# Neighbourhood attention with the scale in the queries' norm, the bias and maxima in PSUM, and the value product turned round

## The reference, cut to what matters

```
q, k, v = split(h @ w_qkv);  q = rms_norm(q, q_g);  k = rms_norm(k, k_g)      # per head
s_loc = (q . k) * 64**-0.5 + bias      # bias: a table by row and column distance,
s_loc = where(col_mask, s_loc, -1e30)  #       -1e30 outside a window of 16 columns
s_ctx = (q . k_c) * 64**-0.5
p = softmax(concat(s_loc, s_ctx))      # 512 probabilities to a query
o = p_loc @ v + p_ctx @ v_c
y = merge(o) @ w_o
```

## Time and profile before

| | |
|---|---|
| median of 3 runs | 1802.4 us |
| lowest, highest | 1801.71, 1804.6 us |
| the profiled execution | 1802.83 us |
| its span | 1801.0 us |
| mean granted TensorE clock | 0.963 of 2.4 GHz |
| PE, PEld busy | 94%, 82% |
| DVE, ACT, POOL busy | 56%, 42%, 5% |
| the attention | from about 1496 to 1572.8 us of the span |

### The profile page before, as it was taken

One profiled execution on the slowest core, in us unless ns is written; L12 is line 12 of the kernel. 1 busy time (PEld: TensorE's weight loads), 2 busy tenths in 40 slices (PEclk: granted clock), 3 DMA queues, 4 the chain that ended last, 5 costly groups with the idle time before them and its releaser, 6 DMA issues.

```text
span 1801.0 us, 29404 instructions
## 1 busy us (share of the span) xinstructions
PE 1685.1 (94%) x11903; PEld 1476.6 (82%) x11903; DVE 1000.8 (56%) x1205; ACT 749.6 (42%) x1100; POOL 95.8 (5%) x70
## 2 busy tenths in 40 slices
PE   6989999989989999959998999999979998789998
PEld 6988998979979989858786888888858784589998
DVE  5687556557785665464246443444353228866574
ACT  4444554344445544344225332233233234645453
POOL 0110000002000000020002000000020101110000
PEclk9999999989999999969998999999989998989999
DMA  7665665756756656612122323332323323145753
GB/s 241 214 208 189 210 204 174 252 177 210 231 174 205 211 190 212 231 45 94 47 70 70 94 72 94 111 95 79 88 94 117 100 71 71 24 128 172 205 173 120
DMA packets 329970, 259.69 MB, mean 144 GB/s; under 512 B 24018, under 2 KB 322386, under 8 KB 329827
## 3 DMA queue, kind: packets, MB, share of 16 engines
q1 hardware_dynamic: 311184, 251.55, 43.9%
q10 hardware_dynamic: 18642, 6.18, 1.6%
HBM read 256.65 MB, written 1.05 MB: 143 GB/s over the span
## 4 chain that ended last, share of the span: by engine, by line
PE 82%; DVE 10%; ACT 4%; issue 1%; POOL 1%; DMA 1%; ACTq 0%; SPq 0%; DVEq 0%
PE banks_g L1013 39%; PE banks_g L763 22%; PE banks_g L753 4%; PE banks_g L1001 3%; PE banks_g L785 2%; ACT near_p L1584 1%; PE bank_s L880 1%; PE bank_m L799 1%; DVE near_p L2006 1%; DVE near_max L2173 1%; PE bank_t L893 1%; DVE w_lo L1726 1%; POOL h L1662 1%; PE banks_g L745 1%; PE bank_o L907 1%
## 5 line engine op out<-in xcount | busy, mean ns | idle before, releaser
L1013 PE MATMUL banks_g<-h_hi,w_lo 128*128 128x512 f32 (+1 forms) x864 | 299.3, 346 | 9.7 <-DVE h_lo L2109 9.7
L1013 PE MATMUL banks_g<-h_lo,w_hi 128*128 128x512 f32 (+1 forms) x864 | 297.4, 344 | 0.0
L1013 PE MATMUL banks_g<-h_hi,w_hi 128*128 128x512 f32 (+1 forms) x864 | 297.3, 344 | 0.0
L1979 DVE TENSOR_TENSOR w_lo<-raw,w_hi 128x2048 fp32r<-128x2048 f32 (+1 forms) x100 | 207.7, 2077 | 158.5 <-ACT w_hi L1378 158.5
L1726 DVE TENSOR_TENSOR w_lo<-raw,w_hi 128x2048 fp32r<-128x2048 f32 x92 | 210.7, 2290 | 103.2 <-ACT w_hi L1219 103.2
L763 PE MATMUL banks_g<-h_hi,w_lo 128*128 128x256 f32 x832 | 241.3, 290 | 8.4 <-DVE h_lo L1967 8.4
L763 PE MATMUL banks_g<-h_lo,w_hi 128*128 128x256 f32 x832 | 236.2, 284 | 0.0
L763 PE MATMUL banks_g<-h_hi,w_hi 128*128 128x256 f32 x832 | 235.8, 283 | 0.0
L1378 ACT ACTIVATE w_hi<-raw 128x2048 fp32r<-128x2048 f32 (+1 forms) x100 | 173.3, 1733 | 74.1 <-DMA raw<-w_down 47.9
L1013 PEld LDWEIGHTS banks_g<-h_hi,w_lo 128*128 128x128 f32 x864 | 163.9, 190 | 33.6 <-DVE h_lo L2109 12.0
L1219 ACT ACTIVATE w_hi<-raw 128x2048 fp32r<-128x2048 f32 x96 | 182.9, 1905 | 6.9 <-issue 2.4
(11 more groups left out here) (306 smaller groups left out, 2907.0 us busy)
## 6 DMA issues: line engine op xcount, KB each, us to landing
raw<-w_in SPq DMA_DIRECT2D x76, 1024.0 KB, 5.1
ada_raw<-ada_w SPq DMA_DIRECT2D x48, 1024.0 KB, 7.2
raw<-w_up SPq DMA_DIRECT2D x88, 512.0 KB, 4.6
raw<-w_down SPq DMA_DIRECT2D x32, 704.0 KB, 4.4
raw<-w_branch SPq DMA_DIRECT2D x12, 1024.0 KB, 5.1
raw<-qkv SPq DMA_DIRECT2D x12, 1024.0 KB, 4.9
raw<-w_out SPq DMA_DIRECT2D x8, 1024.0 KB, 5.0
raw<-even_in SPq DMA_DIRECT2D x6, 1024.0 KB, 5.1
```

Source lines behind the costliest of these rows:

```text
L1013: last = nc.tensor.matmul(gb[:, m * SEQ:m * SEQ + nt], w[:, c, m0:m0 + P], a[:, c, 0:nt], start=c == 0 and n == 0, stop=c == kcs - 1 and n ...
L1979: nc.vector.tensor_tensor(w_lo[:, u % SLOTS, 0:n], raw[:, u % SLOTS, 0:n], w_hi[:, u % SLOTS, 0:n].bitcast(F32), ALU.subtract).then_inc(dv ...
```

## The change

Five things, in one edit:

1. The scale 1/8 moves into the queries' norm: the root is taken of sum + 64 eps in place of sum/64 + eps, for the queries alone.
2. The bias is added to the local scores in place in PSUM. The pass over the context scores goes. The maximum is taken from PSUM, and the exponentials read PSUM and write SBUF. So a score bank pair is free only after the exponentials (PE waits for `near exp` in place of `near masked`).
3. The probabilities are turned as they are, not normalised. The reciprocal is kept (4 buffers).
4. In the value product the turned probabilities (128 keys x 128 queries) are the stationary operand, and `v_n` (128 keys x 64 features) streams. The result is queries x features of both heads, in columns 0 to 127 of its bank.
5. VectorE multiplies that result (128 x 128) by the reciprocal into `near_o`; a new step **near back** on TensorE transposes it into columns 128 to 255 of the same bank, from where `f_hi` and `f_lo` are made as before. The pipeline is one batch deeper: scores b, turn b-2, back b-4, values b-3, exp b.

```diff
-    for b in range(19):
+    for b in range(20):
         if b < 16:
             order.append(("near scores", b))
         if 2 <= b <= 17:
             order.append(("near turn", b - 2))
-        if b >= 3:
+        if b >= 4:
+            order.append(("near back", b - 4))
+        if 3 <= b <= 18:
             order.append(("near values", b - 3))
@@ TensorE
                     if b >= 2:
-                        pe.wait_ge(dve_steps, dve_.at(f"near masked{b - 2}"))
+                        pe.wait_ge(act_steps, act_.at(f"near exp{b - 2}"))
...
-                    pe.wait_ge(dve_steps, dve_.at(f"near probs{b}"))
+                    pe.wait_ge(act_steps, act_.at(f"near exp{b}"))
...
-                    for kt in range(4):
-                        for e in range(2):
-                            hh = 2 * c + e
-                            last = nc.tensor.matmul(ob[64 * e:64 * e + 64, 0:P], v_n[:, kt, hh * HD:hh * HD + HD],
-                                                    near_pt[:, b % 2, kt, e, :], start=kt == 0, stop=kt == 3)
+                    for e in range(2):
+                        hh = 2 * c + e
+                        for kt in range(4):
+                            last = nc.tensor.matmul(ob[:, 64 * e:64 * e + 64], near_pt[:, b % 2, kt, e, :],
+                                                    v_n[:, kt, hh * HD:hh * HD + HD], start=kt == 0, stop=kt == 3)
...
+                elif what == "near back":
+                    b, = arg
+                    pe.wait_ge(dve_steps, dve_.at(f"near o{b}"))
+                    ob = bank_o if b % 2 == 0 else bank_g[0]
+                    nc.tensor.transpose(ob[:, P:2 * P], near_o[:, b % 2, :], ident[:, :]).then_inc(
+                        pe_steps, pe_.step(f"near back{b}"))
@@ ScalarE
-                        nc.scalar.activation(m_root[0:16, 0:nt], bank_m[0:16, 0:nt], ACT.Sqrt, scale=1.0 / HD,
-                                             bias=eps[0:16, 0:1]).then_inc(act_steps, act_.step(f"root{x}"))
+                        by, e_ = (1.0, eps_hd) if x == "q" else (1.0 / HD, eps)
+                        nc.scalar.activation(m_root[0:16, 0:nt], bank_m[0:16, 0:nt], ACT.Sqrt, scale=by,
+                                             bias=e_[0:16, 0:1]).then_inc(act_steps, act_.step(f"root{x}"))
...
                     act.wait_ge(dve_steps, dve_.at(f"near max{b}"))
+                    if b >= 3:
+
+                        act.wait_ge(pe_steps, pe_.at(f"near turn{b - 3} 1"))
                     for e in range(2):
-                        nc.scalar.activation(near_p[b % 3][:, e, :], near_p[b % 3][:, e, :], ACT.Exp,
+                        nc.scalar.activation(near_p[b % 3][:, e, :], near_banks(b)[:, e, :], ACT.Exp,
...
-                        ob[:, 0:P], ACT.Copy).then_inc(act_steps, act_.step(f"near hi{b}"))
+                        ob[:, P:2 * P], ACT.Copy).then_inc(act_steps, act_.step(f"near hi{b}"))
@@ VectorE
-                nc.vector.tensor_tensor(near_p[b % 3][:, :, :], near_p[b % 3][:, :, :],
-                                        near_inv[:, :].rearrange("p (e o) -> p e o", o=1).to_broadcast([P, 2, 512]),
-                                        ALU.mult).then_inc(dve_steps, dve_.step(f"near probs{b}"))
...
-                    nc.vector.scalar_tensor_tensor(pb[:, :, 0:SEQ], sbk[:, :, 0:SEQ], SCALE, backwards(bt),
-                                                   ALU.mult, ALU.add).then_inc(dve_steps, dve_.step("near"))
-                    nc.vector.tensor_scalar(pb[:, :, SEQ:512], sbk[:, :, SEQ:512], SCALE, None, ALU.mult).then_inc(
+                    nc.vector.tensor_tensor(sbk[:, :, 0:SEQ], sbk[:, :, 0:SEQ], backwards(bt), ALU.add).then_inc(
                         dve_steps, dve_.step(f"near masked{b}"))
+                    own()
+                    nc.vector.tensor_reduce(near_max[:, b % 2, :], sbk[:, :, :], AX.X, ALU.max, negate=True).then_inc(
+                        dve_steps, dve_.step(f"near max{b}"))
                     if b:
-                        near_normalize(b - 1)
-                    own()
-                    nc.vector.tensor_reduce(near_max[:, b % 2, :], pb[:, :, :], AX.X, ALU.max, negate=True).then_inc(
-                        dve_steps, dve_.step(f"near max{b}"))
+                        near_reciprocal(b - 1)
...
                 elif what == "near values":
+                    b, = arg
+                    ob = bank_o if b % 2 == 0 else bank_g[0]
+                    dve.wait_ge(pe_steps, pe_.at(f"near values{b}"))
+                    dve.wait_ge(dve_steps, dve_.at(f"near inv{b}"))
+                    nc.vector.tensor_tensor(near_o[:, b % 2, :].rearrange("p (e n) -> p e n", e=2),
+                                            ob[:, 0:P].rearrange("p (e n) -> p e n", e=2),
+                                            near_inv[:, b % 4, :].rearrange("p (e o) -> p e o", o=1).to_broadcast([P, 2, HD]),
+                                            ALU.mult).then_inc(dve_steps, dve_.step(f"near o{b}"))
```

More of the change, by code:

```diff
@@ L397, in program @@
         eps = sb("eps", [P, 1])
+        eps_hd = sb("eps_hd", [P, 1])
         x_t = sb("x_t", [P, KC, SEQ])
@@ L1594, in _ @@
                                                                              act_.step(f"near turned{b} {hf}"))
-                elif what == "near values":
+                elif what == "near back":
                     b, = arg
                     qt, c = divmod(b, KC)
-                    act.wait_ge(pe_steps, pe_.at(f"near values{b}"))
+                    act.wait_ge(pe_steps, pe_.at(f"near back{b}"))
                     ob = bank_o if b % 2 == 0 else bank_g[0]
@@ L1616, in _ @@
             nc.gpsimd.memset(eps[:, :], EPS).then_inc(pool_steps, pool_.step("eps"))
+            nc.gpsimd.memset(eps_hd[:, :], EPS * HD).then_inc(pool_steps, pool_.step("eps"))
             nc.gpsimd.memset(ones[:, :], 1.0).then_inc(pool_steps, pool_.step("ones"))
@@ L1999, in hidden_low, with near_reciprocal @@
                                         ).then_inc(dve_steps, dve_.step(f"f lo{ly} {i}"))
-            def near_normalize(b):
+            def near_reciprocal(b):
                 dve.wait_ge(act_steps, act_.at(f"near exp{b}"))
-                nc.vector.reciprocal(near_inv[:, :], near_sum[:, b % 2, :]).then_inc(dve_steps, dve_.step("near inv"))
-                own()
-                nc.vector.tensor_tensor(near_p[b % 3][:, :, :], near_p[b % 3][:, :, :],
-                                        near_inv[:, :].rearrange("p (e o) -> p e o", o=1).to_broadcast([P, 2, 512]),
-                                        ALU.mult).then_inc(dve_steps, dve_.step(f"near probs{b}"))
+                nc.vector.reciprocal(near_inv[:, b % 4, :], near_sum[:, b % 2, :]).then_inc(
+                    dve_steps, dve_.step(f"near inv{b}"))
             u = 0
@@ L2160, in _ @@
                     qt, c = divmod(b, KC)
[L2161 removed]
+                    sbk = near_banks(b)
                     dve.wait_ge(pool_steps, pool_.at(f"windowed{b // 2}"))
@@ L2165, in _ @@
                     bt = bias[b // 2 % 3][:, 2 * (c % 2):2 * (c % 2) + 2, :]
[L2166 to L2168 removed]
+                    nc.vector.tensor_tensor(sbk[:, :, 0:SEQ], sbk[:, :, 0:SEQ], backwards(bt), ALU.add).then_inc(
                         dve_steps, dve_.step(f"near masked{b}"))
+                    own()
+                    nc.vector.tensor_reduce(near_max[:, b % 2, :], sbk[:, :, :], AX.X, ALU.max, negate=True).then_inc(
+                        dve_steps, dve_.step(f"near max{b}"))
                     if b:
[L2171 to L2174 removed]
+                        near_reciprocal(b - 1)
                     if b == 15:
[L2176 removed]
+                        near_reciprocal(b)
                 elif what == "near values":
+                    b, = arg
[6 more added lines that the diff above has]
+                                            ALU.mult).then_inc(dve_steps, dve_.step(f"near o{b}"))
+                elif what == "near back":
                     b, = arg
@@ L2182, in _ @@
                     dve.wait_ge(act_steps, act_.at(f"near hi{b}"))
-                    nc.vector.tensor_tensor(v8(f_lo), ob[:, 0:P], v8(f_hi).bitcast(F32), ALU.subtract).then_inc(
+                    nc.vector.tensor_tensor(v8(f_lo), ob[:, P:2 * P], v8(f_hi).bitcast(F32), ALU.subtract).then_inc(
                         dve_steps, dve_.step(f"near lo{b}"))
```

6 lines of the change are left out of this document (2 added, 4 removed).

## The result

The change takes **1789.82 us** (median of 4 executions, 1783.28 to 1792.13) against 1803.39 for the kernel before on the same chip: ratio 0.992, 95% interval 0.9892 to 0.9947. The profiled one, 1783.28 us, is the lowest of the four, so what its trace shows beyond the attention is more than the median has.

A forecast was written before the change was run, and what follows sets the result against it. The prediction took a ScalarE-VectorE loop, 4.26 us a batch, to bound the attention and TensorE, 3.92, to follow. The attention's 6.2 us less 0.9 for the clock gave -5.3: 1797.1 us against the median, range 1793.5 to 1803.5.

The forecast's parts named there:

- the sum: TensorE's work in one attention batch, scores to values, added to 3.92 us and becoming the bound against 4.26 to 4.35.
- the load pitch: Value product: loads of 128 columns follow each other every 0.111 us, so sixteen take 1.78 where they took 0.85.
- PSUM cost VectorE nothing extra: Bias and maximum in PSUM take VectorE 0.68 and 1.22 us; the rival of double cost, 1805, had chance 0.02.
- near back found its product ready: Transpose back on TensorE: 0.11 us, its product made some 2 us before, except at the very end.
- The rival of a worse pitch or a leak at each transpose: Value products at pitch 0.126 cost 3.8 us more, waits at transposes back 3.2: 1799 to 1803; chance 0.26.
- The scale and the 64 eps cost nothing: the same root with another constant: Queries' norm: moving the scale into the root was priced at no time.
- all of the gain passes to the end: Stages after the attention: bound by TensorE with weights split in advance, so the attention's 5.3 us reach the total.
- The allowance for the clock, 0.9 us: Batches without scores: a clock fall costing some 1.7 us, given half a chance and taken off the 6.2 gain.
- The slower clock: Rival in batches 3 to 15: TensorE's clock falls to half, a batch takes 7.8 us, 1807 to 1842; chance 0.12.
- The load is not the bound: Rival in the value product: loads keep the old 0.05 pitch, TensorE needs 3.0, gain 18 us, 1784; chance 0.03.
- The Trainium skill's rule against the edit: Value product: tiling by columns, the removed form, is up to twice as fast; without it 0.85 becomes 1.7 us.
- the loop bounds the kernel before: Attention before: exponentials, product with the reciprocal and maximum wait in a ScalarE-VectorE loop, 4.26 us a batch, 4.35 on average.

The follow-up runs named there:

- Without the shift: The change with the new constant in a second column of the tile of `eps`, so no other tile moves: 1798.51 us, ratio 0.9967.
- the kernel with 128 columns: The change with 128 columns of `v_n` streamed behind each load of the value product instead of 64, mixing the heads' sums: 1789.15 us, ratio 0.9917.
- the tiled form: The change with the value product of before (64 columns of `v_n` loaded, probabilities streaming), normalising by the wrong rows: 1777.43 us, ratio 0.9854.
- its first half alone: The change with VectorE normalising probabilities in two one-scalar passes, the old value product and no near back: 1776.89 us, ratio 0.9855.
- the last experiment: The kernel before with the maximum of b moved ahead of the product for b-1 and four reciprocal buffers: 1800.29 us, ratio 0.9983.
- the shifted kernel before: The kernel before with 32 bytes left free behind `eps` and nothing else changed: 1795.34 us, ratio 0.9948.
- the two-halves version without the shift: The change with VectorE's two one-scalar passes, old value product, no near back, and the constant in the tile of `eps`: 1790.39 us, ratio 0.9928.

## Why the prediction was wrong

- **The attention: right in its mechanism and its size.** TensorE became the bound at 3.92 us a batch, exactly the sum; the load pitch was 0.111; PSUM cost VectorE nothing extra (0.70 and 1.22); near back found its product ready; from first scores to `w_o` 6.3 us went, by the working 6.2. The rival of a worse pitch or a leak at each transpose is out with that. Without the shift the change gains 5.1; the text said 5.3. Around the loop two small errors nearly cancel, which is luck: scores 4 start 13.3 us after the first scores, where the text had 14.0, since the half clock of the start lasted some 3.4 us and not 5.6; from there to `w_o` it took 57.2 where the text had 56.7.
- **Slips in the working**, none of which made the miss: 1503.7 + 3.7 + 2.8 is 1510.2, not 1509.9; and the first rival's two prices, 3.8 and 3.2, are together more than the gain of 5.3, so it reaches to 1804 and not only to 1803.
- **The failed step** is in the costing of the change's first edit, "The scale and the 64 eps cost nothing: the same root with another constant", and with it the step "all of the gain passes to the end", which took every stage outside the attention as untouched. The root does cost nothing. But the other constant has a tile, and the 32 bytes that it takes move all tiles allocated after it, which changes the distance from matmul to matmul in stages that the change doesn't edit (0.1175 to 0.1133 us in the last feed-forward). Measured alone they are worth 8.3 us (0.9948), more than the whole of the attention. Why the place of a tile does that stays open. The sum had no term for it, and no row of before could have priced it; the diff showed that a tile was added, though, and a term of unknown size on both sides would have widened the range.
- **The allowance for the clock, 0.9 us, was not needed**: the clock stays at 1.00 through the batches without scores. Without it the forecast would be 1 us nearer.
- **The slower clock** didn't come: 1.00 from 1500 to 1560. In the Trainium skill, TensorE: Matmul & The Clock Gate, PE-mode transpose says that transposes do not count as work for the gate. Transposes are 0.59 + 0.44 + about 0.1 of a batch's 3.92 us here, and the clock held, from 1552 to 1554 even without scores; what transposes alone would do no run here shows.
- **"The load is not the bound" named 1784**, nearer to the result than the forecast, and is still false. The pitch of 0.111 and the kernel with 128 columns both refuse it. A time that fits is no evidence for a mechanism.
- **The Trainium skill's rule against the edit** (TensorEngine Tiling (Array Packing), When to Use Tiling) was weighed as a matter of size, and the runs give it more weight: going back to the tiled form saves 0.71 us a batch and 12 us in all. The change is faster than before in spite of its second half; its first half alone, with VectorE's product split in two, has 27 us with the shift and 12.8 without.
- **Half right:** that the loop bounds the kernel before. It does, but VectorE's own work stands just beneath it (4.09 in the last experiment). The 4.35 on average against 4.26 in an even batch has a second source, VectorE's product stretched beside GpSimd (2.17 at 1515.28).

## What to carry to other kernels

When a change adds or resizes any tile, look at what moves behind it, and make one control in which only the addresses move before crediting the algorithm. When a loop through two engines is cut, add up what each engine still has to do: here the gain was set by TensorE's 3.92, and the work moved onto that engine (the turned product) gave back 12 of the 18 us that the attention could have gained. A product by a per-row number can go behind the maximum on the same engine, in one-scalar form, before it is worth moving to another one.

## What the hardware showed beyond what was expected

- The distance of matmuls of 256 columns at full clock changes when the streamed tiles move in SBUF and the weight slots don't. In the last feed-forward it is 0.1175 us as in the kernel before, 0.1133 with 32 bytes more (while the faster rate holds), 20/169 = 0.118 with 96; in the first network's run of 96 from `h_hi` it is 0.1176, 0.1187 with 32 bytes more and 0.1209 with 64. Those of 512 columns took 200/856 = 0.234 us before and 200/884 = 0.226 with 96 bytes.
- In the last feed-forward the kernels shifted by 32 bytes run at 172 or 179 records in 20 us and go from one to the other within an execution, at the same clock. DMA traffic doesn't tell them apart: in the shifted kernel before, 172 stand beside 186 GB/s and 179 beside 134. What throws the switch stays open. Executions of these kernels lie 3 to 11 us apart and those of before at most 7, but those of the two-halves version without the shift lie 10 apart, so the spread is no sure sign of it.
- VectorE's passes from SBUF were stretched beside GpSimd's addition in SBUF: the product of 1024 took 1.23 us alone and 2.17, 2.21 and 3.23 where they met, a pass of 512 by one scalar 0.48 alone and once 2.65. In the change the bias addition, in place in PSUM, took 0.69 to 0.70 and the maximum from PSUM 1.22 in all sixteen batches, and no batch of its loop is longer than 3.93. That PSUM is the reason wasn't tested alone.
- VectorE multiplies 512 columns in SBUF by one scalar for each partition at 0.88 us for two, where one such pass with its source in PSUM took 0.68. Over the whole attention the mean of one is 0.570: 30 of the 32 take 0.47 to 0.49, and two, beside GpSimd's addition, 1.08 and 2.65.
- Loads of 128 x 128 have the same pitch of 0.111 us with 64 and with 128 columns streamed behind each.
